# Adding up x1's squares on GpSimd instead of VectorE, in a one-layer hybrid block

## What is computed

```
def rmsnorm(x, g):
    y = x * rsqrt(mean(x * x, axis=-1) + EPS)
    return y * g

def reference(x, ...):
    y = hybrid_mixer(rmsnorm(x, norm_mix_pre), ...)
    x = x + rmsnorm(y, norm_mix_post)              # this sum is x1
    h = rmsnorm(x, norm_ffn_pre)
    y = conv_gated_mlp(h, w_gate, w_up, conv_ffn_w, conv_ffn_b, w_down)
    return x + rmsnorm(y, norm_ffn_post)
```

## Time and profile before

| what | us |
| --- | --- |
| median of three runs | 2149.89 |
| lowest and highest of them | 2149.03, 2150.46 |
| the profiled execution's own time | 2149.89 |
| its span, first to last instruction | 2148.1 |
| PE busy in it | 2116.0 (99%) |
| DVE busy | 1685.9 (78%) |
| ACT busy | 1017.9 (47%) |
| POOL busy | 346.8 (16%) |

### The profile page before, as it was taken

How to read it: one execution, slowest core, us unless ns; L and a number is a source line. 1 busy time by engine, 2 the same in 40 slices (tenths; PEclk the granted TensorE clock), 3 DMA queues, 4 the chain that set the end, 5 groups by cost and what they waited for, 6 DMA issues and landing times.

```text
span 2148.1 us, 44222 instructions
## 1 busy us (share of the span) xinstructions
PE 2116.0 (99%) x18226; PEld 2091.2 (97%) x18226; DVE 1685.9 (78%) x2298; ACT 1017.9 (47%) x1281; POOL 346.8 (16%) x431
## 2 busy tenths in 40 slices
PE   9999999999999999999999999999999999999995
PEld 8999999999999999999999999999999999999995
DVE  7777777778855877888888888888887767768886
ACT  6555554456322554444444444444444545445442
POOL 0222222222100001111111111211212001112003
PEclk9999999999999999999999999999999999999997
DMA  5788989888543436888878888787888658679544
GB/s 178 171 187 208 207 188 207 196 188 188 162 123 98 156 108 184 221 224 214 218 218 216 222 225 214 219 216 215 247 211 272 190 167 277 179 190 300 177 142 169
DMA packets 238755, 423.84 MB, mean 197 GB/s; under 512 B 17009, under 2 KB 151793, under 8 KB 237313
## 3 DMA queue, kind: packets, MB, share of 16 engines
q0 software_dynamic: 88224, 159.97, 35.9%
q1 hardware_dynamic: 147776, 256.84, 35.8%
q10 hardware_dynamic: 2592, 4.72, 0.6%
HBM read 382.64 MB, written 89.16 MB: 220 GB/s over the span
## 4 chain that ended last, share of the span: by engine, by line
PE 93%; DVE 3%; issue 1%; ACT 1%; POOL 1%; DMA 1%; POOLq 0%; DVEq 0%; ACTq 0%
PE bank L2073 29%; PE bank L2075 29%; PE bank L2074 29%; PE bank L2457 2%; PE bank L2152 1%; PE bank L2165 1%; DVE w_all L1219 1%; DMA act_lo_f<-t_spill 1%; PE bank L2177 0%; PE bank L2176 0%; ACT act_hi L1140 0%; ACT w_all L771 0%; PE bank L2237 0%; POOL act_lo_f L762 0%; POOL tsum_f L762 0%
## 5 line engine op out<-in xcount | busy, mean ns | idle before, releaser
L2073 PE MATMUL bank<-act_hi,w_all 128*128 128x256 f32 x3272 | 910.1, 278 | 4.8 <-DVE w_all L1219 2.2
L2074 PE MATMUL bank<-act_lo,w_all 128*128 128x256 f32 x3272 | 903.8, 276 | 0.0
L2075 PE MATMUL bank<-act_hi,w_all 128*128 128x256 f32 x3272 | 903.8, 276 | 0.0
L2073 PEld LDWEIGHTS bank<-act_hi,w_all 128*128 128x128 f32 x3272 | 614.3, 188 | 11.2 <-issue 3.7
L2074 PEld LDWEIGHTS bank<-act_lo,w_all 128*128 128x128 f32 x3272 | 614.4, 188 | 0.7 <-issue 0.2
L2075 PEld LDWEIGHTS bank<-act_hi,w_all 128*128 128x128 f32 x3272 | 614.4, 188 | 0.0
L2073 PE MATMUL bank<-tsum,w_all 128*128 128x256 f32 x1280 | 353.5, 276 | 0.0
L2075 PE MATMUL bank<-tsum,w_all 128*128 128x256 f32 x1280 | 353.3, 276 | 0.0
L2074 PE MATMUL bank<-tsum,w_all 128*128 128x256 f32 x1280 | 353.3, 276 | 0.0
L1134 ACT ACTIVATE w_all<-raw_s 128x1024 fp32r<-128x1024 f32 x172 | 182.7, 1062 | 243.3 <-PE bank L2075 222.7
L1219 DVE TENSOR_TENSOR w_all<-raw,w_all 128x1024 fp32r<-128x1024 f32 x134 | 164.0, 1224 | 133.6 <-ACT w_all L771 131.6
(11 more groups left out here) (390 smaller groups left out, 3513.0 us busy)
## 6 DMA issues: line engine op xcount, KB each, us to landing
raw<-weights SPq DMA_DIRECT2D x262, 512.0 KB, 4.4
w_sums<-weights POOLq DMA_DIRECT2D x96, 512.0 KB, 7.0
raw_s<-weights SPq DMA_DIRECT2D x84, 512.0 KB, 5.7
raw_s<-weights POOLq DMA_DIRECT2D x84, 512.0 KB, 5.8
raw_a<-weights SPq DMA_DIRECT2D x66, 512.0 KB, 5.7
raw_s<-w_sums SPq DMA_DIRECT2D x48, 512.0 KB, 5.0
t_spill<-h_out POOLq DMA_DIRECT2D x48, 256.0 KB, 3.7
act_lo_f<-t_spill POOLq DMA_DIRECT2D x11, 1024.0 KB, 9.1
```

What stands on the lines that cost most here:

```text
L2073: pe.matmul(dst, ah, bh, start=start, stop=False, skip_group_check=goes_on)
L2074: pe.matmul(dst, ah, bl, start=False, stop=False, skip_group_check=goes_on)
L2075: return pe.matmul(dst, al, bh, start=False, stop=stop, skip_group_check=goes_on)
```

## The change

GpSimd takes over the 15 adds. They stand in its list after the loads of the residual and ahead of its first store of hidden tiles; add k waits for the square of tile k and for its own add before. DVE's function `add_x1_squares` and its three calls are gone. PE waits for 15 increments of `x1sum_ready` in place of one. The adds have the same shapes and the same operands, `acc`, `og[:, 0]` and `og[:, k]`.

```
@@ GpSimd, after the residual's loads
             for k in range(KT):
                 pool.wait_ge(unit_used, N_OUT + max(k, 6))
                 pool.dma_start(x1[:, k], xT[:, k]).then_inc(res_landed, 16)
+
+            for k in range(1, KT):
+                pool.wait_ge(x1sq_done, k + 1)
+                at_least(pool, x1sum_ready, k - 1)
+                pool.tensor_tensor(acc[:], og[:, 0] if k == 1 else acc[:], og[:, k], ALU.add).then_inc(x1sum_ready, 1)
@@ VectorE, after the stage of x1
-            def add_x1_squares(k0, k1):
-
-                for k in range(k0, k1):
-                    dve.wait_ge(x1sq_done, k + 1)
-                    ins = dve.tensor_tensor(acc[:], og[:, 0] if k == 1 else acc[:], og[:, k], ALU.add)
-                    chain(ins) if k < KT - 1 else ins.then_inc(x1sum_ready, 1)
-
             split(N_FF + 8, 0)
-            add_x1_squares(1, 6)
             split(N_FF + 9, 1)
-            add_x1_squares(6, 11)
             split(N_FF + 10, 0)
-            add_x1_squares(11, KT)
@@ TensorE
             def x1_sum():
-                pe.wait_ge(x1sum_ready, 1)
+                pe.wait_ge(x1sum_ready, KT - 1)
                 channel_sum(SB[2], acc[:])
```

## The result

The changed kernel takes 2161.52 us (median of 6 runs, 2160.89 to 2162.56) against 2150.18 for the kernel before in the same comparison: 11.3 us or 0.55% slower, a ratio of 1.0055 with a 95% interval of 1.0043 to 1.0066. The profiled execution's span is 2159.0 us, 10.9 more than the 2148.1 of the earlier trace rows. The forecast was 2159.9, in a range of 2153.8 to 2164.0.

What follows compares the result with a forecast made beforehand. PE bounds the kernel, with DVE nearly as full in the stage of x1. DVE's delay 13.2 less slack 3.1 gives 10.1, rounded to 10.0; span 2148.1 + 10.0 = 2158.1, with 1.8 around it 2159.9; range 2153.8 to 2164.

Steps and rivals of the forecast that it cites:

- The removal at 0: Stage of x1: taking 15 adds, 10.3 us in all, off DVE gains 0, since they delay nobody.
- PE's wait, GpSimd's list, the queues: 0: Behind the stage: PE's wait for 15 increments, and stores and loads queued around the adds on GpSimd, cost 0.
- The exclusion: Stage of x1: a GpSimd add holds DVE instructions with both inputs in SBUF for 1.12 us, not those with one in PSUM.
- The delay of DVE, 13.2 us: Stage of x1: 14 adds hold DVE, 11 x 1.06 + 3 x 0.5 = 13.2 us; the 15th costs nothing.
- eleven full and three cheap ones: Stage of x1: 11 adds cost DVE 1.06 us each, 3 falling on a scaling cost 0.5 each.
- The slack, 3.1 us: Stage of x1: DVE's waits, about 2.0 us, and its lead of 1.1 come off the delay before it reaches PE.
- a lead of 1.1 us: End of the stage: DVE's last but one low part ends at 751.78, PE needs it at about 752.86.
- The pace, 7.2 us a unit, stops below 2 us: Stage of x1: a unit of two tiles takes about 7.2 us instead of 5.44, PE standing still for 1.8.
- Hiding: Rival: the exclusion is peculiar to the program's end, the adds run under the stage, time stays 2149.9; 10%.
- partial exposure: Rival: only part of DVE's instructions in the stage are held, L1224 being exempt; 3.9 us, about 2153.8; 8%.
- The clock: Rival: PE's stops in the stage also lower its granted clock, 2 to 4 us more, 2162 to 2164; 8%.
- The gain: Rival: relieving DVE shortens PE's waits for splits at 776 to 812 us, up to 2.0 us, 2147.9; 4%.

Runs made afterwards that it cites:

- the runs with seven adds: Against the changed kernel, only the first or last seven adds on GpSimd in the stage, DVE adding the rest behind it: 2154.76 us; 2152.55 us, one run.

## Why the prediction was right

**The removal at 0.** Right. With no adds anywhere the stretch grew by 0.09 us and the time did not fall.

**PE's wait, GpSimd's list, the queues: 0.** Right. PE shows no wait for GpSimd in the changed kernel, and the wait ahead of the reciprocal is unchanged at 4.64 us.

**The exclusion.** Right, and shown rather than argued by the runs: it takes GpSimd reading SBUF (memsets cost nothing) beside a DVE instruction with two SBUF inputs (the scalings have no spread), at a place where DVE has no room (the adds behind the stage leave it untouched). Two collisions at the end of the program had given 1.12 us for the hold, and 1.06 for its net cost; the full holds in the stage are 1.04 to 1.09. These holds, and not the time, speak against a hold of the whole 1.26 us of an add, for which the prediction gives a sum of 12.2: the measured 11.3 lies between that and 10.0.

**The delay of DVE, 13.2 us.** Measured 13.04 us in 14 holds. The division into eleven full and three cheap ones was near it too: ten of 1.04 to 1.09, and four of 0.75, 0.37, 0.83 and 0.38.

**The slack, 3.1 us.** This is the term that was off. It was summed from a lead of 1.1 us and 2.0 of waits; the change swallowed 1.4. That makes 11.7 us from the first low part to the reciprocal; this execution entered the stage 0.4 us earlier than the one of before, so its reciprocal came 11.3 later, and the medians say 11.3 too, where 10.0 was forecast. Both parts were read too large.

The waits were 0.23 us and up to 0.1 more in each of six or seven units. That is the spare time of a unit, and it shows as a wait in two units only, the two of the earlier trace rows. The other splits of the stage in the kernel before (DVE in time):

```profile
721.96 1.23 DVE L1219 TENSOR_TENSOR w_all<-raw,w_all 128x1024 fp32r<-128x1024 f32 x1 [0.28 <-ACT w_all L771]
727.08 1.22 DVE L1219 TENSOR_TENSOR w_all<-raw,w_all 128x1024 fp32r<-128x1024 f32 x1
732.20 1.23 DVE L1219 TENSOR_TENSOR w_all<-raw,w_all 128x1024 fp32r<-128x1024 f32 x1
...
748.58 1.22 DVE L1219 TENSOR_TENSOR w_all<-raw,w_all 128x1024 fp32r<-128x1024 f32 x1
```

The first one's wait of 0.28 us is no slack: it is still there, at 0.27, in the changed kernel. From it to 732.20 the splits start 5.12 us apart, DVE's own pace, without a wait. At the start of the stage PE waits for DVE (0.4 us for a low part in the earlier trace rows), so there is no lead then; DVE builds it in these units, and waits only once it is there. The forecast counted the spare time of these units as waits, and then once more as the lead.

The lead was put at 1.1 us, from the start of ACT's copy at 752.86. PE's own row is earlier:

```profile
752.60 0.28 PE L2073 MATMUL bank<-act_hi,w_all 128*128 128x256 f32 x1
```

That is the first matmul of the last unit. In the changed kernel PE starts 0.15 us behind the end of the low part that it waits for (762.80 and 0.74 long, then 763.69). So the one that was ready at 751.78 could have been 0.7 us later, and no more. Two waits of 0.24 and 0.23, with the prediction's 0.1 more for each, and 0.7 of lead make 1.3 us, and 1.4 was swallowed. This is worked out from the two traces afterwards; the runs with seven adds agree in direction, 0.89 swallowed early and 1.28 late. DVE's visible waits in the stage fell only from 1.96 to 1.23 us, since most of those at its first tiles are for ACT and stay.

**The pace, 7.2 us a unit, stops below 2 us.** Measured 7.25, the longest stop 1.7. PE's waits in the stage come to 8.7 and 0.9 us in ten stops, close to the forecast of about 10, but they understate the loss for the reason found above: with 0.17 us more a stop, and less the one stop of 0.4 in the kernel before, they make 10.7.

**The rivals.** Hiding and partial exposure fall: the scalar_tensor_tensor and the instructions that write fp32r are held as much as the plain one. The clock stayed at 1.00 through all stops of the stage, up to 1.7 us each, so that rival did not come about. The Trainium skill (TensorE: Matmul & The Clock Gate, "The HAM clock gate") reports a kernel in which short waits between groups of matmuls made the clock swing; the ten stops of this stage, of 1.7 us at most, did not. The gain did not come by relieving DVE. It was to be had at the place that the rival named, 776 to 812 us, but through the other side of the chain, by an earlier product on PE.

## What to carry to other kernels

Before moving elementwise work from VectorE to GpSimd, look at what VectorE does at the time the moved work will run: two SBUF inputs there and a read here exclude each other, and in a stage where VectorE has no room every microsecond of GpSimd's reading is one of the program, unless it is started beside instructions with an operand in PSUM. Count slack once: spare time that builds a lead shows as no wait, so add to the lead only waits that stand in the rows, and read the rows of every unit for them. And ask first whether the work moved delays anybody: here 10 us of adds were free, and half a unit in the place of one product was worth more than all of them.

## What the runs showed of the hardware

The exclusion is not told by the length of GpSimd's row. An add of 128x512 took 1.29 to 1.30 us beside a scaling and held for 1.04 to 1.09; a tensor_scalar of 128x512, with one input, took 1.49 to 2.00 us and held a low part for 0.35. GpSimd is held in its turn: behind the stage an add that met a split of 1.23 us took 2.16 us, 0.87 more than its own 1.29.

Adds on GpSimd that wait for one another came every 1.37 us behind the stage where no split stood beside them, against 1.23 for the independent adds at the end of the program.

After a stop, PE's matmuls start further apart for a while. In the changed kernel's PE in time, behind the last stop of the stage, they are 0.118 us apart for some 25 matmuls, where a PE that has not stopped has 0.113:

```profile
763.69 0.35 PE L2068 MATMUL bank<-act_hi,w_all 128*128 128x256 f32 x1 [0.59 <-DVE act_lo L1229]
763.88 0.28 PE L2069 MATMUL bank<-act_lo,w_all 128*128 128x256 f32 x1
764.00 0.28 PE L2070 MATMUL bank<-act_hi,w_all 128*128 128x256 f32 x1
764.12 0.28 PE L2068 MATMUL bank<-act_hi,w_all 128*128 128x256 f32 x1
```
